# Modulation columns summed on TensorE from eight weight pieces, with the first two weight chunks interleaved

## The reference, cut to what matters

```
h   = silu(c) @ ada_w + ada_b                 # shift and scale are its first 2 * 1024 columns
x_n = x * rsqrt(mean(x * x) + eps) * norm1_g
h1  = x_n * (1 + scale) + shift               # 2048 x 1024
z   = h1 @ w_in                               # 2048 x 2048, in 16 chunks of 128 columns
```

## Time and profile before

| | |
|---|---|
| Median of 3 runs | 3113.48 us (3108.71 to 3115.22) |
| Profiled execution | 3116.04 us |
| Its span | 3114.2 us |
| PE busy | 91% of the span |
| Columns (L1567) on PE | start 37.72 us |
| First product | 58.89 us |

### The profile page before, as it was taken

One profiled execution on the slowest core, in us unless ns is written; L12 is line 12 of the kernel. 1 busy time (PEld: TensorE's weight loads), 2 busy tenths in 40 slices (PEclk: granted clock), 3 DMA queues, 4 the chain that ended last, 5 costly groups with the idle time before them and its releaser, 6 DMA issues. The chain is left out here.

```text
span 3114.2 us, 41252 instructions
## 1 busy us (share of the span) xinstructions
PE 2835.8 (91%) x13492; PEld 2200.2 (71%) x13493; DVE 1987.2 (64%) x3104; ACT 1464.4 (47%) x2353; POOL 388.2 (12%) x289
## 2 busy tenths in 40 slices
PE   4999997999999997899997898996899999999996
PEld 3767666676777766788874677885677777777774
DVE  6657995554546365543462565346888888888874
ACT  4414563554545453332243333212666666666663
POOL 3101221000000000110110000110122212222221
PEclk9999998999999998998997999997999999999998
DMA  6274325131221206411126998443989997877774
GB/s 234 94 257 187 92 81 162 41 116 58 82 92 53 100 28 238 132 51 45 45 68 218 281 315 301 162 169 135 330 285 298 358 364 258 277 244 220 259 253 142
DMA packets 292202, 554.80 MB, mean 178 GB/s; under 512 B 32089, under 2 KB 98905, under 8 KB 288482
## 3 DMA queue, kind: packets, MB, share of 16 engines
q1 hardware_dynamic: 273666, 492.06, 45.6%
q0 software_dynamic: 14400, 52.44, 6.9%
q10 hardware_dynamic: 4000, 8.53, 0.9%
HBM read 418.21 MB, written 143.15 MB: 180 GB/s over the span
## 5 line engine op out<-in xcount | busy, mean ns | idle before, releaser
L2593 DVE TENSOR_TENSOR moe_w_lo<-moe_W,moe_w_hi 128x1024 fp32r<-128x1024 f32 x384 | 460.7, 1220 | 86.6 <-ACT moe_w_hi L2521 71.8
L2521 ACT CAST moe_w_hi<-moe_W 128x1024 fp32r (+1 forms) x384 | 401.9, 1053 | 152.5 <-PE moe_h1b L2444 75.9
L1559 PE MATMUL project_bank<-h_lo,w_hi 128*128 128x512 f32 x512 | 204.1, 399 | 0.0
L515 DVE TENSOR_SCALAR_CACHE_REDUCE att_S<-att_bank 128x512 f32<-128x512 f32 x192 | 125.0, 689 | 120.3 <-PE att_bank L303 120.3
L336 PE MATMUL att_bank<-h_hi,w_hi 128*128 128x512 f32 x384 | 171.2, 446 | 14.5 <-PEq L137 11.2
L2469 PE MATMUL moe_yb<-moe_W,moe_hT 128*128 x384 | 172.9, 593 | 0.0
L2442 PE MATMUL moe_h1b<-moe_w_hi,moe_xT_hi 128*128 128x512 f32 x384 | 156.0, 406 | 4.8 <-DVE moe_xT_lo L2604 4.8
L421 ACT ACTIVATE att_S<-att_S,att_nm 128x128 f32<-128x128 f32 (+15 forms) x128 | 154.1, 1205 | 0.0
L338 PE MATMUL att_bank<-h_hi,w_lo 128*128 128x512 f32 x384 | 152.5, 397 | 0.0
L337 PE MATMUL att_bank<-h_lo,w_hi 128*128 128x512 f32 x384 | 152.4, 397 | 0.0
L2444 PE MATMUL moe_h1b<-moe_w_hi,moe_xT_lo 128*128 128x512 f32 x384 | 151.3, 394 | 0.0
(11 more groups left out here) (478 smaller groups left out, 6963.2 us busy)
## 6 DMA issues: line engine op xcount, KB each, us to landing
moe_W<-in_moe_w SPq DMA_DIRECT2D x96, 2048.0 KB
w_raw<-in_gate_w SPq DMA_DIRECT2D x48, 512.0 KB, 3.9
out_sg<-gateT SPq DMA_DIRECT2D x32, 768.0 KB, 11.1
gateT<-att_gates SPq DMA_DIRECT2D x48, 256.0 KB, 2.4
gateT<-gate_out SPq DMA_DIRECT2D x48, 256.0 KB, 2.4
early<-in_ada_w SPq DMA_DIRECT2D x8, 1024.0 KB, 9.2
project_spare<-in_x SPq DMA_DIRECT2D x16, 512.0 KB, 6.1
w_raw<-in_w_in SPq DMA_DIRECT2D x16, 512.0 KB, 4.3
```

The source lines that it names most:

```text
L1559: pe.matmul(bank[n % 4][:], w_hi[b][:, k, :], low[:, k, at512(tb)], start=False, stop=False)
L2521: nc.scalar.copy(w_hi[:, slot(p, first), :], raw(at, p)).then_inc(q["w13_high"], 1)
L2593: nc.vector.tensor_tensor(w_lo[:, own, :], raw(at, p), w_hi[:, own, :].bitcast(F32), ALU.subtract).then_inc(q["w1_low" if p < 4 else "w3_l ...
```

## The change

- `add(k)` and `sums` are gone. `column_piece(k)` on PE takes each piece as it is: 16 matmuls that load a 128 x 128 block of `early[k]` as weights and stream one column of `ccol`, accumulated in bank 0 over the eight pieces.
- `ada_b` and `norm1_g` come as rows (1 x 1024, three DMAs) instead of columns, and PE turns them: one matmul of zeros that opens the bank, and 24 that load a 1 x 128 piece of a row as weights and stream a single 1.0. DVE then copies two results out of the bank and makes the scale in a third step.
- DVE scales the first four x tiles, not one of them. ACT's squares of tiles 4 to 7 move from ahead of `col_ready` into the turning loop.
- Four turns stand between the pieces 4, 5 and 6, so that four banks are filled when `col_ready` comes. In the loop, `pair(n - 5)` runs one k of a unit of chunk 0 and of one of chunk 1 after turn n, from n = 5.
- Weight chunk 1 is loaded into the room of `early[0]` and no longer waits for the split of chunk 0.

```diff
     def on_dve(i):
-        return i % 4 == 3
+        return i < 4 or i % 4 == 3
...
                 sp.dma_start(g["ccol"][:], g["c"].rearrange("a (k p) -> p (a k)", p=P), allow_slow_non_contiguous=True).then_inc(f["c_ready"], 16)
-                for k in range(4):
+                load_early(0)
+                load_x(0)
+                for to, frm in ((shift_row, g["ada_b"][:, 0:D]), (scale_row, g["ada_b"][:, D:W]), (norm_row, g["norm1_g"])):
+                    sp.dma_start(to, frm).then_inc(f["line"], 16)
+                for k in range(1, 4):
                     load_early(k)
                     load_x(k)
-                sp.dma_start(bcol[:], g["ada_b"][:, 0:W].rearrange("a (k p) -> p (a k)", p=P), allow_slow_non_contiguous=True).then_inc(f["consts"], 16)
-                sp.dma_start(n1[:], g["norm1_g"].rearrange("a (k p) -> p (a k)", p=P), allow_slow_non_contiguous=True).then_inc(f["consts"], 16)
                 sp.dma_start(g["consts"][:], g["const_pack"]).then_inc(f["consts"], 16)
-                for k in range(4, AR):
+                for k in range(4, KD):
                     load_early(k)
                 load_w(0)
-                sp.wait_ge(f["added"], 1)
-                load_early(AR)
+                sp.wait_ge(f["piece_used"], 1)
+                load_w(1)
...
-                pe.wait_ge(f["consts"], 48)
-                pe.wait_ge(f["added"], KD)
-                for k in range(2 * KD):
-                    mm = pe.matmul(bank[0][:, k:k + 1], sums[:, k * P:(k + 1) * P], const(g, "ones")[:, 0:1], start=True, stop=True)
-                mm.then_inc(f["col_summed"], 1)
-                for n in range(KD):
+                def column_piece(k):
+
+                    pe.wait_ge(early_ready[k], 16)
+                    for j in range(2 * KD):
+                        mm = pe.matmul(bank[0][:, j:j + 1], early[k][:, j * P:(j + 1) * P], g["ccol"][:, k:k + 1], start=False, stop=k == KD - 1 and j == 2 * KD - 1)
+                    mm.then_inc(f["col_summed"] if k == KD - 1 else f["piece_used"], 1)
+
+                def pair(m):
+
+                    tb, k = m // KD, m % KD
+                    for c in range(2):
+                        products(2 * tb + c, k, k + 1)
+
+                pe.wait_ge(f["line"], 48)
+                pe.wait_ge(f["seeded"], 2)
+                pe.matmul(bank[0][:, 0:3 * KD], norm_row[:, 0:P], nil, start=True, stop=False)
+                for a, of in enumerate((shift_row, scale_row, norm_row)):
+                    for k in range(KD):
+                        pe.matmul(bank[0][:, a * KD + k:a * KD + k + 1], of[:, k * P:(k + 1) * P], one, start=False, stop=False)
+                pe.wait_ge(f["c_made"], 1)
+                for k in range(KD):
+                    column_piece(k)
+                    if k == 4:
+                        pe.wait_ge(f["consts"], 16)
+                    if k in (4, 5):
+                        turn(2 * (k - 4))
+                        turn(2 * (k - 4) + 1)
+                for n in range(4, NT8):
                     turn(n)
-                pe.wait_ge(f["col_ready"], 1)
-                for n in range(KD, NT8):
-                    turn(n)
-                    tb, k = n // KD - 1, n % KD
-                    products(2 * tb + k // 4, k % 4 * 2, k % 4 * 2 + 2)
+                    if n >= 5 and n - 5 < KD * (TB - 1):
+                        pair(n - 5)
...
                 split(0)
-                for i in range(4, 8):
-                    square_x(i)
                 split(1)
                 act.wait_ge(f["col_ready"], 1)
                 for n in range(NT8):
                     tb, k = n // KD, n % KD
                     high_x(n)
-                    if 1 <= tb < TB - 1 and k < 4:
+                    if tb < TB - 1 and k < 4:
                         square_x(4 * (tb + 1) + k)
...
-                link(nc.vector.tensor_tensor(ccol[:], ccol[:], cexp[:], ALU.mult))
-                for k in range(KD):
-                    add(k)
-                    if k == 6:
-                        for i in range(4):
-                            scale(i)
+                nc.vector.tensor_tensor(ccol[:], ccol[:], cexp[:], ALU.mult).then_inc(f["c_made"], 1)
+                dve.wait_ge(f["c_made"], 1)
+                for i in range(4):
+                    scale(i)
                 split(0)
-                dve.wait_ge(f["consts"], 48)
+                split(1)
+                dve.wait_ge(f["consts"], 16)
                 dve.wait_ge(f["col_summed"], 1)
-                link(nc.vector.tensor_tensor(col[:], bank[0][:, 0:2 * KD], bcol[:], ALU.add))
-                nc.vector.scalar_tensor_tensor(col[:, KD:], col[:, KD:], 1.0, n1[:], ALU.add, ALU.mult).then_inc(f["col_ready"], 1)
+                link(nc.vector.tensor_copy(n1[:], bank[0][:, 2 * KD:3 * KD]))
+                link(nc.vector.tensor_copy(col[:, 0:KD], bank[0][:, 0:KD]))
+                nc.vector.scalar_tensor_tensor(col[:, KD:], bank[0][:, KD:2 * KD], 1.0, n1[:], ALU.add, ALU.mult).then_inc(f["col_ready"], 1)
                 dve.wait_ge(f["col_ready"], 1)
-                split(1)
```

More of the change, by code:

```diff
@@ L1332, in stage_project @@
     ROW_AT = (16, 20, 24, 27)
-    XR, AR, W = 8, 7, 2 * D
-    early = [rooms[i // 4][:, i % 4 * W:(i % 4 + 1) * W] for i in range(AR + 1)]
-    sums = early[AR]
+    XR, W = 8, 2 * D
+    early = [rooms[i // 4][:, i % 4 * W:(i % 4 + 1) * W] for i in range(KD)]
+    raw1 = early[0][:, 0:KD * P].rearrange("p (k n) -> p k n", k=KD)
     def pieces_by(n):
@@ L1345, in on_dve, with raw_of @@
     def on_dve(i):
-        return i % 4 == 3
+        return i < 4 or i % 4 == 3
+    def raw_of(c):
+        return raw1 if c == 1 else raw[:]
     with Stage(nc, "project") as s:
@@ L1364, in stage_project @@
         brow = sq[0:1, :]
-        cexp, bcol, n1 = s.sb("cexp", [P, KD]), s.sb("bcol", [P, 2 * KD]), s.sb("n1", [P, KD])
+        shift_row, scale_row, norm_row = o_hi[0:1].rearrange("p a n -> p (a n)"), o_lo[0:1].rearrange("p a n -> p (a n)"), oz[0:1].rearrange("p a n -> p (a n)")
+        cexp, n1 = s.sb("cexp", [P, KD]), s.sb("n1", [P, KD])
+        seed = s.sb("seed", [P, 32])
+        nil, one = seed[0:1, 0:3 * KD], seed[0:1, 3 * KD:3 * KD + 1]
         col, ss = s.sb("col", [P, 2 * KD]), s.sb("ss", [P, NT])
@@ L1370, in stage_project @@
         q = {n: s.sem(n) for n in names}
-        front_names = ("c_ready consts exped col_summed col_ready squared rooted reduced scaled_pool scaled_dve turned h_high raised h_split added").split()
+        front_names = ("c_ready c_made consts line seeded w1_ready exped piece_used col_summed col_ready squared rooted reduced scaled_pool scaled_dve turned h_high raised h_split").split()
         f = {n: s.sem(f"x_{n}") for n in front_names}
-        early_ready = [s.sem(f"early_ready{i}") for i in range(AR)]
+        early_ready = [s.sem(f"early_ready{i}") for i in range(KD)]
         x_ready = [s.sem(f"x_ready{i}") for i in range(XR)]
@@ L1386, in load_early @@
                 def load_early(k):
-                    sp.dma_start(early[k % AR], g["ada_w"][0][k * P:(k + 1) * P, 0:W]).then_inc(early_ready[k % AR], 16)
+                    sp.dma_start(early[k], g["ada_w"][0][k * P:(k + 1) * P, 0:W]).then_inc(early_ready[k], 16)
                 def load_x(i):
@@ L1393, in load_w @@
                     src = w_in[:, :, chunks[c][1] * P:(chunks[c][1] + 1) * P] if c < NC else gate_w[:, :, (c - NC) * P:(c - NC + 1) * P]
-                    sp.dma_start(raw[:], src).then_inc(q["raw_ready"], 16)
+                    sp.dma_start(raw_of(c), src).then_inc(f["w1_ready"] if c == 1 else q["raw_ready"], 16)
                 def load_ada(m):
@@ L1444, in _ @@
                                          allow_slow_non_contiguous=True).then_inc(q["small"], 16)
-                sp.wait_ge(q["w_split"], 2)
+                sp.wait_ge(q["w_split"], 1)
                 load_w(2)
@@ L1488, in _ @@
                     sp.wait_ge(qk_stored[b], 32 * NU // 4)
-                sp.wait_ge(q["raw_ready"], 16 * (NC + 2))
+                sp.wait_ge(q["raw_ready"], 16 * (NC + 1))
                 sp.wait_ge(q["row_stored"], 64)
@@ L1497, in _ @@
                 nc.gpsimd.memset(half_pi[:], math.pi / 2).then_inc(q["biased"], 1)
+                nc.gpsimd.memset(nil, 0.0).then_inc(f["seeded"], 1)
+                nc.gpsimd.memset(one, 1.0).then_inc(f["seeded"], 1)
                 for i in range(NT):
@@ L1538, in turn @@
                     if k == 0:
-                        pe.wait_ge(f["scaled_pool"], 3 * tb + 3)
-                        pe.wait_ge(f["scaled_dve"], tb + 1)
+                        if tb >= 1:
+                            pe.wait_ge(f["scaled_pool"], 3 * tb)
+                            pe.wait_ge(f["scaled_dve"], 4 + tb)
+                    if tb == 0 and k < 4:
+                        pe.wait_ge(f["scaled_dve"], 4)
                     if n >= 4:
@@ L1604, in split @@
                 def split(c):
```

(9 more changed lines are left out.)

2 lines of the change are left out of this document (removed).

## The result

The changed kernel takes 3142.26 us (median of 7, 3130.29 to 3146.66) against 3114.29 us of before (median of 7, 3108.71 to 3115.22). The ratio is 1.0085, 95% interval 1.007 to 1.010: slower by 0.85%, small but clear of the noise. Forecast were 3146 us and a range of 3138 to 3154. The profiled execution took 3139.70 us, its span is 3137.8 us. Among the experiments one execution of dve_sums (10541 us, mean granted clock 0.54) and one of dve_sums_wide (9186 us, 0.40) ran in a far slower state; their ratios leave these out, the medians given do not and would be 0.3 us lower without them.

A forecast was written before the change was run, and what follows sets the result against it. PE was taken to bound the kernel, so its exit from the front decides: 32.5 + 1.5 - 2.3 + 0.8 = +32.5 us on 3116.04 gives 3148.5, 3146 as median; range 3138 to 3154.

The forecast's parts named there:

- Price and count of the loads: Front column stream on PE: 322 weight loads at 0.215 us, 69.2 us, putting the first raise 32.5 us later.
- The start: PE's first load: begins at 8.3 us, when the three bias and norm rows land; bounds about 4 and 18.8.
- late-rows rival: Start of PE's stream: rows land at 18.8 us like single elements, +10.5 us, time 3156; chance 4%.
- The first rival: Front column stream: runs at full clock, 0.10 us a load, time 3109 to 3111; chance 4%.
- The second: Front column stream: clock rises in the first turns after piece 4, -12 us, time 3134; chance 6%.
- The loop: Turning loop, first raise to unit 6: its terms net zero, bounds -5 and +3; unit 6 60 to 62 us after.
- Turn 8: Turning loop: ACT's squares there delay POOL's first tile, +1.5 us; turn 8 comes 13 to 14 us after first raise.
- PE would lose what it saved at the end of the loop: Loop's end: 4.2 us from 18 moved products becomes waiting for DVE's last low tile; rival that it is kept, 8%.
- The clock at turn 8: Turning loop: products under the wait for POOL put PE at full clock at turn 8, -2.3 us.
- the longer wait: Start of unit 6: after a wait of 5 to 6 us PE runs longer at 0.50, +0.8 us.
- The sum: Whole kernel: front and loop terms together +32.5 us, giving 3146 us; holds as worked out with 78%.

The follow-up runs named there:

- dve_sums: Changed kernel with DVE again scaling and adding the eight pieces and PE summing the result in 16 column matmuls; 3111.03 us, ratio 0.9978 against the kernel before.
- dve_sums_wide: Kernel with DVE's sums restored, plus eight wide zero matmuls behind the bias rows and two behind the first turns; 3111.14 us, ratio 0.9974 against before.
- warm_start: Changed kernel plus six fp32 128 x 512 matmuls on zeros at PE's start, result unused; 3144.14 us, ratio 1.0080 against the kernel before.
- pieces_only: Kernel before with one part alone: PE takes the eight pieces directly, 256 weight loads, old bias path and loop kept; 3128.12 us, ratio 1.0043.
- no_pairs: Changed kernel with the old turning loop, six products behind each turn from turn 8 on, none earlier; 3145.02 us, ratio 1.0089 against the kernel before.
- held_clock: Changed kernel plus wide zero matmuls: six at the start, one ahead of each bias row and every eight columns; 3174.09 us, ratio 1.0186 against before.
- row_stream: Changed kernel with column-sum operands exchanged: one column of c as weights, pieces streamed through, finished rows turned by 16 matmuls; 3118.18 us, ratio 1.0008 against before.
- change_again: The changed kernel run once more, unaltered; 3147.34 us over 4 executions, ratio 1.0096 against the kernel before.

## Why the prediction was right

- **Price and count of the loads.** 322 loads at 0.215 us were forecast from 8.3 to 77.5 us; they ran from 8.18 to 76.9, 0.213 each. That the printed 1.00 was not to be believed was the step on which all hung, and warm_start shows it (0.213 us a load at a recorded 0.50). A one-partition weight load cost as much as a full one: 16 in 3.55 us.
- **The start.** The three rows landed by 8.18 us; the late-rows rival (18.8) did not come.
- **The first rival** (full clock) is refuted by warm_start and pieces_only. The rule of the Trainium skill, TensorE: Matmul & The Clock Gate, Part 1, that sustained activity releases the throttle, does not hold for this stream: 68.7 us of loads without a gap did not raise the clock (after), and a stream that had it lost it (warm_start). By that rule the change would have ended at 3109 to 3111, as the rival's sum has it. **The second** (a rise after piece 4) did not come either: pieces 5 to 7 still took 6.8 us each.
- **The loop.** Unit 6 came 60.4 us behind the first raise, in the 60 to 62 of the forecast. Turn 8 was 0.7 us earlier than worked out. That PE would lose what it saved at the end of the loop is shown: its wait grew from 2.24 (no_pairs) to 6.27 us and ends with the last low tile. The clock at turn 8, forecast at 2.3 us, brought 2.0 in the first profile and 0.5 in the repeat, where the clock fell again behind it; that the term came out so near was in part luck. Behind the longer wait PE stayed at 0.50 until 143.8, 5.8 us against 3.3 before, which is about 1.2 us of time by estimate where 0.8 was put; in the repeat, behind a wait of 6.45 us, it was 3.1 us and cost nothing over before. So neither term of the clock is a fixed price.
- **The sum was 1.3 us over at unit 6; the rest of the miss lies behind the front.** From unit 6 on PE has the same list in both, yet the profiled stretches differ by 6.8 us there. Windows of before (the first fence) and of the change, 1000 us, 500 us and the rest behind unit 6, columns as in rows 3; read the column of the granted clock:

```profile
107.60:1107.60 1000.00, 924.90 (x4774) 695.21 (x4775) 598.87 (x1063) 475.73 (x898) 54.62 (x32) 0.98 0.33 108
1107.60:1607.60 500.00, 460.04 (x2328) 377.31 (x2328) 252.37 (x558) 177.23 (x393) 51.09 (x21) 0.93 0.26 88
1607.60:3114.20 1506.60, 1390.79 (x6090) 1076.84 (x6088) 1060.81 (x1385) 757.75 (x970) 244.69 (x216) 0.95 0.76 253
```

```profile
138.00:1138.00 1000.00, 926.13 (x4741) 697.71 (x4742) 597.19 (x1056) 473.90 (x894) 54.64 (x32) 0.97 0.33 107
1138.00:1638.00 500.00, 459.92 (x2374) 376.67 (x2373) 256.51 (x566) 180.03 (x398) 51.24 (x21) 0.95 0.26 89
1638.00:3137.80 1499.80, 1389.49 (x6077) 1076.01 (x6075) 1058.43 (x1383) 757.77 (x970) 245.06 (x216) 0.96 0.76 254
```

The first stretch has a mean clock of 0.98 and 0.97, the middle one of 0.93 and 0.95, the rest of 0.95 and 0.96: the difference changes its sign from place to place. Summed from the clock's record of each trace, with the stretch behind unit 6:

```
               us at 0.50   stretch, us
no_pairs         228.6        3000.2
after            231.6        2999.8
pieces_only      232.4        3002.7
dve_sums         236.8        3001.6
held_clock       237.6        3009.2
dve_sums_wide    237.9        3006.1
row_stream       241.3        3006.1
before           241.8        3006.6
change_again     245.4        3006.8
warm_start       259.2        3013.7
```

A microsecond at 0.50 goes with about half a microsecond of time: reckoned so from the first profile of the change, held_clock lies 6.4 us above and all others within 3.2 us, so that change_again's 0.1 is closer than the rule is good for. Of the 6.8 us between before and the change this gives 5.1. Nothing is given back at a fixed place. How long the clock is low differs from execution to execution of one kernel, and the time goes with it: the changed kernel's seven times go from 3130.29 us at a mean clock of 0.966 to 3146.66 at 0.960. The forecast put this stretch at 0.8 us more than before and no scatter on it; of the 3.7 us by which the median is under the forecast, the front explains 1.3. Two of the seven executions, at 3130 us, lie under the forecast's range, and the repeat's median is 3147.34: the mechanism of the front is shown, while a miss as small as 3.7 us is smaller than this scatter and owes something to luck. Why the falls lie where they do was not tried and stays open.

## What to carry to other kernels

A sum over partitions by matmul costs a weight load for each 128 x 128 block that goes in as weights: sum first on an idle engine and load once (32 loads, dve_sums). If PE must take the big operand as it is, let it stream through a one-column weight: at the same clock a piece costs the same (6.8 or 3.4 us), but here the wide matmuls got the full clock and the weight loads did not (30.5 us instead of 54.6 for the same 8 MB). When a stream of loads looks twice as dear as elsewhere, compare the spacing with a stretch of known clock before believing a printed clock ahead of its first record. Work moved earlier on an engine that later waits for another brings only what it does to that wait: ask what is the limit at the end of the loop.

## What the runs showed that was not expected

- PE busy without a gap is no protection of the clock: 57.90 of 57.90 us busy at 0.50 (warm_start), and 17.00 of 17.00 with a wide matmul ahead of every eight columns (held_clock).
- Wide matmuls ahead of a short column sum were worth 0.6 us of the 3.5 hoped for: the clock fell 0.9 us into the column loads (dve_sums_wide). PE had waited 1.68 us for DVE just ahead of them, so that these loads alone brought it down is not shown.
- DVE's scaling of an x tile took 0.75 us while POOL was idle (dve_sums, 25.82 us) and 1.42 us in the change at 88.17, while POOL scaled a tile from 87.72 to 90.78. The Trainium skill, SBUF — State Buffer, SBUF: two separate sides, says that DVE and GpSimd share a port pair that one of them locks for a whole instruction; a block of POOL's whole 3.06 us is not seen, but the time nearly doubled.
